# A fused decoder layer on one core: the recurrence's preparation begun 12 slots earlier, its steps spaced wider, and the expert sums cut into four quarters

## The chip, the cores and the metric

One core of a Trainium2 chip runs the whole kernel. The metric is the device time of one execution in microseconds, lower being better. The kernel before took 3550.49 us, the median of three runs (3546.98 to 3573.14).

## What is computed

One decoder layer over 1024 tokens of width 1024, all in float32:

```python
a = rms_norm(h, norm_mix_g)
z = a @ w_in                                   # columns: recurrence 1792, convolution 1024, gates 2048
o_r = rwkv7_branch(z_rwkv, ...)                # recurrence over time, 8 heads of 64
o_c = conformer_conv_branch(z_conv, ...)       # 31 taps, depthwise, layer norm, silu
h = h + (g_r * o_r + g_c * o_c) @ w_out
# expert part: per token 8 heads x 16 chosen experts out of 16384
coef = gates * gelu(einsum('cd,ced->ce', c, u_tab[idx]))
h = h + einsum('ce,ced->cd', coef, v_tab[idx])
h = h + sigmoid(rms_norm(h) @ ple_w_gate) * (p @ ple_w_proj)
return rms_norm(h, final_norm_g)
```

Before the recurrence its inputs are prepared: decay and `a` through small up-projections and sigmoids, the normed key direction `kk`, the running sums of the decay's logarithm inside a chunk of 64 tokens and their exponentials, and a bonus term. The recurrence itself is solved chunk by chunk with matrix products (an inverse of a triangular matrix by squaring), 16 steps for each chunk.

## The kernel before

The 1024 tokens are 8 tiles of 128. The main loop has 10 periods `t` of 128 slots `s` (`SLOTS`), one slot for each expert row of a token. In period `t`:

- GpSimd gathers, in each slot, one row of 4 KB for each of 128 tokens out of `u_tab` for tile `t` (`gather_u`, L986) and one out of `v_tab` for the tile before (`gather_v`, L994, 12 slots late). Each gather is 512 KB. It waits until the buffer it goes to is free; there are 4 to 6 buffers for u and 5 to 8 for v.
- VectorE multiplies the u row with the tile's activations and sums it (`dot`, L2248), one in each slot. Slot 0 of a period is where its first `dot` stands, and the 128 `dot`s mark the slots in the trace.
- TensorE adds one v row block in each slot (`add_tokens`, L1325). The product has 32 output rows, so it fills one of four strips of 32 columns of the array and 32 partitions of the accumulator `acc`. Each is made as two halves of 512 columns, the second on the strip `lane ^ 2`. At the end of a tile VectorE adds `acc` to the residual, putting the strips back in place (`summed`, L2257, slot 12, `SUM_ROWS`).
- Between these, the next tile's front is computed, spread over the same slots by tables and constants (`front(t + 1, s)` on each engine). The preparation (`prep`) stands in slots 0 to 17 (`PREP_AT` for VectorE; slots 2, 5, 9 on TensorE; slots 0, 3, 6, 8, 12 on ScalarE). The recurrence (`rec`) stands in slots 20 to 63: two chunks of 15 entries, one entry each 1.5 slots (`rec_step`), TensorE and ScalarE in the entry's slot and VectorE in the one behind. The 124 convolution taps (`conv_tap`, L1968) of tiles 3 to 7 stand partly (44, `EARLY_TAPS`) one a slot from slot 84 of the period before, the other 80 in slots 0 to 65. From slot 66 come the mixing products with streamed weights, w_out, the turned activations, the queries (slots 104 to 113) and the first scores.
- In periods 1 to 3 TensorE also computes the input projection of the last 512 tokens (`late_product`, L1413). In period 7 there is no front; the tails of the first tiles (gate product, final norm) stand in its place. Periods 8 and 9 only add v rows and do the last tails.

Every engine runs its instructions strictly in the order in which the loops write them, so a wait in one slot holds all that stands behind it on that engine. What ties the engines together are the gathers: the u gather of slot `s` waits for a `dot` some slots back, the v gather for an `add_tokens` some slots back, and both stand in one queue on GpSimd.

The preparation's `p_kk` and `p_nrm` lie in `actT` before, where the next tile's queries read too; `pi` is the PSUM tile `pd` (two banks of 512), which preparation, recurrence, queries and mixing share.

```python
def rec_step(s):
    j = -(-2 * (s - REC_AT) // 3)
    return divmod(j, REC_PE - 1) if s >= REC_AT and j < REC_STEPS and REC_AT + 3 * j // 2 == s else None
```

## Time and profile before

| | us |
|---|---|
| median of 3 runs (lowest to highest) | 3550.49 (3546.98 to 3573.14) |
| the profiled execution's own time | 3567.71 |
| its span, first to last instruction | 3566.0 |
| TensorE busy | 2750.9 (77%) |
| VectorE busy | 2363.7 (66%) |
| GpSimd busy | 1964.6 (55%) |
| ScalarE busy | 531.5 (15%) |
| bytes moved, mean rate | 1246.47 MB, 350 GB/s |
| mean granted TensorE clock | 0.855 |

The profiled execution is 1.71 us longer than its span and 17 us longer than the median of the runs. Busy times are of one engine's own instructions; waits are not in them. By the starts of the `dot`s, periods 0 to 7 begin at 243, 544, 968, 1394, 1799, 2186, 2583 and 2974 us of the span, and the last `dot` starts at 3331 us. In the views, stretches given by start and end in us are stretches of slots found in that way.

### The profile page before, as it was taken

How to read it: one execution, taken by the hardware profiler on the slowest of the kernel's cores; microseconds unless marked ns; L12 is line 12 of the kernel's file. 1: busy time of each engine (PE TensorE's matmuls, PEld its weight loads, DVE VectorE, ACT ScalarE, POOL GpSimd, SP SyncE). 2: the span in 40 equal slices, each digit the busy share in tenths (PEclk: the TensorE clock that was granted, in tenths of full speed). 3: DMA queues.
4: the chain of work that ended last, by engine and by line, in shares of the span. 5: the costliest groups of instructions: out<-in, count | busy, mean ns of one | idle time of the engine just before them, and what ended most of it. 6: DMA issues, size and time to landing. Idle time of an engine off the chain costs nothing.

```text
span 3566.0 us, 42043 instructions
## 1 busy us (share of the span) xinstructions
PE 2750.9 (77%) x15556; PEld 1288.3 (36%) x15556; DVE 2363.7 (66%) x6100; ACT 531.5 (15%) x1162; POOL 1964.6 (55%) x2093
## 2 busy tenths in 40 slices
PE   9899886888888889986756676667656777677787
PEld 7777762333323333333323332233223332222111
DVE  5678889676676657766787767867686756665200
ACT  3211311110111102111011101010111101111101
POOL 0013345555655566556665666666665666666663
PEclk9999997999999899998867786678767787798999
DMA  6559998999999999989999999999999999999996
GB/s 218 209 179 306 352 344 305 329 359 377 382 357 322 366 375 377 369 317 403 393 373 335 369 406 368 353 338 407 379 363 332 394 395 403 386 378 396 375 361 234
DMA packets 385293, 1246.47 MB, mean 350 GB/s; under 512 B 40512, under 2 KB 75072, under 8 KB 384320
## 3 DMA queue, kind: packets, MB, share of 16 engines
q0 software_dynamic: 294912, 1073.87, 79.8%
q1 hardware_dynamic: 90176, 169.91, 13.5%
q8 instruction: 123, 2.02, 0.2%
q14 instruction: 82, 0.67, 0.1%
HBM read 1216.75 MB, written 26.87 MB: 349 GB/s over the span
## 4 chain that ended last, share of the span: by engine, by line
PE 36%; DVE 17%; another core or an unknown queue 13%; DMA 13%; issue 11%; POOL 7%; ACT 2%; SPq 0%; POOLq 0%; DVEq 0%; ACTq 0%
PE e_acc L1325 9%; DVE e_u L2248 5%; PE e_pl L1413 5%; DMA e_v<-in_v_tab,e_idxT 4%; DMA e_u<-in_u_tab,e_idx 3%; PE e_pd L1201 3%; PE e_pd L1021 3%; PE e_pd L1227 3%; PE e_acc L1370 3%; POOL e_v L994 3%; PE e_acc L1395 3%; DVE e_late L2248 2%; POOL e_u L986 2%; DMA e_late<-in_v_tab,e_idxT 2%
## 5 line engine op out<-in xcount | busy, mean ns | idle before, releaser
L2248 DVE CUSTOM_DVE_ANT_0 e_u<-e_u,e_c 128x1024 f32<-128x1024 f32 x776 | 942.4, 1215 | 315.8 <-DMA e_u<-in_u_tab,e_idx 240.4
L986 POOL DMA_INDIRECT e_u<-in_u_tab,e_idx x776 | 745.7, 961 | 693.3 <-DVE e_dots L2248 274.6
L994 POOL DMA_INDIRECT e_v<-in_v_tab,e_idxT x711 | 675.6, 950 | 517.4 <-PE e_acc L1325 203.3
L1325 PE MATMUL e_acc<-e_v,e_wd 128*32 128x512 f32 x2844 | 817.3, 699 | 171.6 <-DMA e_v<-in_v_tab,e_idxT 115.0
L1413 PE MATMUL e_pl<-e_late,e_v 128*128 128x512 f32 x608 | 340.8, 658 | 46.5 <-DVE e_side L2058 17.2
L2248 DVE CUSTOM_DVE_ANT_0 e_late<-e_late,e_c 128x1024 f32<-128x1024 f32 x248 | 300.8, 1214 | 102.4 <-DMA e_late<-in_u_tab,e_idx 74.3
L1325 PE MATMUL e_acc<-e_late,e_wd 128*32 128x512 f32 x832 | 271.9, 731 | 73.5 <-DMA e_late<-in_v_tab,e_idxT 47.2
L986 POOL DMA_INDIRECT e_late<-in_u_tab,e_idx x248 | 237.1, 956 | 163.8 <-DVE e_dots L2248 106.2
L1325 PEld LDWEIGHTS e_acc<-e_v,e_wd 128*32 128x32 f32 x2844 | 113.6, 116 | 533.0 <-issue 266.9
L1968 DVE SCALAR_TENSOR_TENSOR e_gbc<-e_hc,e_cw,e_gbc 128x128 f32<-128x128 f32 x960 | 303.6, 344 | 1.5 <-issue 1.0
L994 POOL DMA_INDIRECT e_late<-in_v_tab,e_idxT x208 | 197.3, 948 | 133.2 <-issue 52.8
L1021 PE MATMUL e_pd<-e_arena 64*64 64x64 f32 x3584 | 164.1, 247 | 117.7 <-ACT e_arena L1479 61.3
L1021 PEld LDWEIGHTS e_pd<-e_arena 64*64 64x64 f32 x3584 | 140.2, 156 | 241.2 <-ACT e_arena L1479 105.1
L1413 PEld LDWEIGHTS e_pl<-e_late,e_v 128*128 128x128 f32 x608 | 98.9, 195 | 296.4 <-issue 241.4
L1479 ACT ACTIVATE e_arena<-e_pd 128x512 f32<-128x512 f32 (+1 forms) x192 | 90.5, 471 | 745.4 <-remote 392.0
L1395 PE MATMUL e_acc<-e_v 128*128 128x256 f32 x608 | 153.6, 396 | 19.9 <-DMA e_v<-in_w_in 15.7
L1201 PE MATMUL e_pd<-e_w_out,e_actT 128*128 128x512 f32 x256 | 135.8, 661 | 23.6 <-DVE e_actT L2121 17.7
L1227 PEld LDWEIGHTS e_pd<-e_actT,e_w_q 128*128 128x128 f32 x1024 | 129.5, 204 | 56.2 <-issue 54.0
L1251 PE MATMUL e_ps<-e_keys,e_qT 64*128 64x128 f32 x256 | 78.8, 395 | 89.7 <-remote 60.2
L1227 PE MATMUL e_pd<-e_actT,e_w_q 128*128 128x128 f32 x1024 | 140.3, 293 | 9.5 <-issue 8.9
L1288 PE MATMUL e_pd<-e_w_out,e_actT 128*128 128x512 f32 x256 | 129.5, 637 | 13.1 <-ACT e_actT L1530 12.2
L1395 PEld LDWEIGHTS e_acc<-e_v 128*128 128x128 f32 x608 | 114.9, 197 | 44.2 <-issue 17.1
(299 smaller groups left out, 3249.4 us busy)
## 6 DMA issues: line engine op xcount, KB each, us to landing
e_u<-in_w_in SPq DMA_DIRECT2D x38, 512.0 KB, 3.9
e_v<-in_w_in SPq DMA_DIRECT2D x38, 512.0 KB
e_v<-in_w_in SPq DMA_DIRECT2D x76, 256.0 KB
e_u<-in_u_tab,e_idx POOLq DMA_INDIRECT x776
e_zb<-in_w_c SPq DMA_DIRECT2D x48, 256.0 KB
e_v<-in_v_tab,e_idxT POOLq DMA_INDIRECT x711
e_arena<-in_w_r SPq DMA_DIRECT2D x32, 256.0 KB
e_zb<-in_w_r SPq DMA_DIRECT2D x32, 256.0 KB
```

Source lines behind the costliest of these rows:

```text
L986: pool.indirect_dma_start(out=rows_in[i], out_offset=None, in_=io["u_tab"], in_offset=bass.IndirectOffsetOnAxis(ap=idx[n % 2][:, j:j + 1], ...
L994: pool.indirect_dma_start(out=rows_in[i], out_offset=None, in_=io["v_tab"], in_offset=bass.IndirectOffsetOnAxis(ap=idxT[n % (LAG + 1)][:, ...
L1021: last = pe.matmul(pi[r, out, i * CH:(i + 1) * CH], a[r, i, :], b[r, i, :] if len(b.shape) == 3 else b[r, :], start=True, stop=True)
L1201: last = pe.matmul(pd[:, h * HALF:(h + 1) * HALF], mixt[:, k, :], w_out[:, k, h * HALF:(h + 1) * HALF], start=(k == 0), stop=(k == KT - 1))
L1227: last = pe.matmul(pd[:, h * P:(h + 1) * P], w_q[:, k, h * P:(h + 1) * P], actT[:, k, :], start=(k == 0), stop=(k == KT - 1))
L1288: last = pe.matmul(pd[:, h * HALF:(h + 1) * HALF], actT[:, k, :], w_ple[:, k, h * HALF:(h + 1) * HALF], start=(k == 0), stop=(k == KT - 1))
L1325: last = pe.matmul(acc[rows, cols], w[:, at_:at_ + 32], rows_in[row][:, cols], start=(step == 0), stop=True, skip_group_check=True)
L1370: last = pe.matmul(out, w_a[m % UW][:, k, :], ahead[:, k, 0:n], start=(k == 0), stop=(k == KT - 1))
L1395: last = pe.matmul(acc[:, first:first + BEHIND_T], w_b[i % BW][:, j, :], behind[:, j, :], start=(j == 0), stop=(j == KT - 1))
L1413: last = pe.matmul(pl[:, :], w_late[:, half, in_half, :], late[:, k, :], start=(k == 0), stop=(k == KT - 1))
L1968: dve.scalar_tensor_tensor(out=out, in0=hc[:, i, j:j + P], scalar=col(cw, j * CONV_TILES + i), in1=out, op0=ALU.mult, op1=ALU.add).then_in ...
L2248: dve.tensor_tensor_reduce(rows_in[i], rows_in[i], c[:, :], 1.0, 0.0, ALU.mult, ALU.add, dots[n % 2][:, j:j + 1]).then_inc(s_dot, 1)
```

## The change

Four things are changed together.

1. The preparation of tiles 2 to 7 begins in slot 116 of the period before its old place (`EARLY = 12`): `prep_at(t + 2, s - SLOTS + EARLY)` at the end of each period, and `prep_at(n, s + begins_early(n))` in `front`. Its own order is changed too: the squared key's norm is made first on TensorE, then the reciprocals, then the scans. It is spread over slots 0 to 20 of its own count (`PREP_DVE_AT`), so 12 of them lie before the period's start and the rest in slots 0 to 8. Tiles 0 and 1 keep their period. `p_kk` goes to the arena and `p_nrm` to `zb`, so that neither lies in `actT`. VectorE has 30 instructions for it, not 29.
2. The recurrence of tiles 2 to 7 starts in slot 10, not 20, and still ends in slot 63: its 30 entries are 53/29 = 1.83 slots apart, not 1.5. For tile 1 it runs from slot 22 to 63.
3. `EARLY_TAPS` goes from 44 to 64, two a slot from slot 84 to 115 instead of one a slot from 84 to 127, so 60 instead of 80 are left for slots 0 to 65 of tiles 3 to 7.
4. `add_tokens` makes each v block as four quarters of 256 columns on the four strips (`strip_of` is `lane ^ part`), not two halves of 512 on two. `summed` puts them back with 11 additions (1 of 128 partitions, 4 of 32, 2 of 64, 4 of 32, each 256 wide), not 3 of 512, and the first `add_tokens` of a tile waits for 5 and then for all 11 of them.

```diff
-PREP_AT = {0: 0, 4: 1, 5: 2, 6: 3, 7: 4, 8: 5, 9: 6, 10: 7, 11: 8, 12: 9, 14: 10, 16: 11, 17: 12}
-REC_AT, REC_STEPS = 20, 2 * (REC_PE - 1)
+EARLY = 12
+PREP_PE_AT = {1: 0, 3: 1, 14: 2}
+PREP_ACT_AT = {0: 0, 2: 1, 4: 2, 7: 3, 10: 4}
...
+REC_AT, REC_END, REC_STEPS = 22, 63, 2 * (REC_PE - 1)
-EARLY_AT, EARLY_TAPS = 84, 44
+EARLY_AT, EARLY_TAPS = 84, 64
...
-SUM_ROWS = [((slice(0, P), slice(0, P)),), ((LOW, HIGH), (HIGH, LOW))]
+SUM_ROWS = [((slice(0, P), slice(0, P)),), tuple((STRIPS[i], STRIPS[i ^ 1]) for i in range(LANES)),
+            ((LOW, HIGH), (HIGH, LOW)), tuple((STRIPS[i], STRIPS[i ^ 3]) for i in range(LANES))]
...
+def rec_step(n, s):
+
+    first = REC_AT - begins_early(n)
+    span, last = REC_END - first, REC_STEPS - 1
+    j = -(-(s - first) * last // span)
+    return divmod(j, REC_PE - 1) if 0 <= j <= last and first + span * j // last == s else None
...
-        return range(min(s - EARLY_AT, EARLY_TAPS), min(s - EARLY_AT + 1, EARLY_TAPS)) if s >= EARLY_AT else range(0)
+        return range(min(2 * (s - EARLY_AT), EARLY_TAPS), min(2 * (s - EARLY_AT + 1), EARLY_TAPS)) if s >= EARLY_AT else range(0)
...
-        p_kk, p_nrm = actT[:, 0:PAIRS, :], actT[:, PAIRS:, :]
+        p_kk, p_nrm = part(30, 4, "p (i t) -> p i t", i=PAIRS), zb[:, :, 0, :, 0, :]
...
-                for h in range(D // HALF):
+                for h in range(PARTS):
                     if j == 0 and n:
-                        pe.wait_ge(s_hh, SUMS[NH] * (n - 1) + SUMS[h + 1])
-                    cols = slice(h * HALF, (h + 1) * HALF)
+                        pe.wait_ge(s_hh, SUMMED * (n - 1) + (HALF_SUMMED, SUMMED)[h * PART_W // HALF])
+                    cols = slice(h * PART_W, (h + 1) * PART_W)
...
                     if t + 1 < NT:
                         front(t + 1, s)
+                    if t + 2 < NT and s >= SLOTS - EARLY:
+                        prep_at(t + 2, s - SLOTS + EARLY)
```

VectorE in slots 117 to 121 of period 5. L2248 is the dot (two rows of it in each slot), L1968 a tap, L2156 to L2172 the choice of the best 16 of a head. Before:

```order
L2156 MATCH_REPLACE e_sc<-e_tv,e_sc 128x128
L2157 MATCH_REPLACE e_sc<-e_tv,e_sc 128x128
L2248 ISA e_u,e_dots<-e_u,e_c 128x1024
L2248 ISA e_dots 128x1
L1968 SCALAR_TENSOR_TENSOR e_gbc<-e_hc,e_cw,e_gbc 128x128
L2162 MAX e_tv<-e_sc 128x8 x2
L2248 ISA e_late,e_dots<-e_late,e_c 128x1024
L2248 ISA e_dots 128x1
L1968 SCALAR_TENSOR_TENSOR e_gbc<-e_hc,e_cw,e_gbc 128x128
L2166 MAX_INDEX e_ti<-e_tv,e_sc 128x8 x2
L2167 TENSOR_TENSOR e_onehot<-e_tv 128x256
```

The same engine after, slots 116 to 120 (L2291 is the dot, L1939 to L1947 the preparation of tile 7: the key direction, the norm's lower bound, a reciprocal):

```order
L1939 TENSOR_TENSOR e_arena<-e_arena,e_vec 128x512
L2291 ISA e_u,e_dots<-e_u,e_c 128x1024
L2291 ISA e_dots 128x1
L2232 TENSOR_SCALAR e_half<-e_pos 128x16 x2
L2291 ISA e_u,e_dots<-e_u,e_c 128x1024
L2291 ISA e_dots 128x1
L2235 CAST e_halff<-e_half 128x32
L1943 TENSOR_SCALAR e_zb<-e_pd 128x2x4x64
L2291 ISA e_u,e_dots<-e_u,e_c 128x1024
L2291 ISA e_dots 128x1
L2238 TENSOR_TENSOR e_onehot<-e_halff,e_iota 128x512
L1947 RECIPROCAL e_zb<-e_zb 128x2x64
```

The taps have left these slots and the preparation's instructions have come in.

TensorE from the start of a period on. L1215 turns the activations for the new tile's dots, L1135, L1152 and L1156 are the preparation, L1325 the v sums. Before:

```order
L1325 MATMUL e_acc<-e_v,e_wd 32x512 x4
L1215 MATMUL e_c<-e_ident,e_actT 128x128 x8
L1325 MATMUL e_acc<-e_v,e_wd 32x512 x6
L1135 MATMUL e_pd<-e_arena,e_wa_up 128x128 x8
L1325 MATMUL e_acc<-e_late,e_wd 32x512 x4
L1325 MATMUL e_acc<-e_v,e_wd 32x512 x2
L1251 MATMUL e_ps<-e_keys,e_qT 128x128 x2
L1135 MATMUL e_pd<-e_arena,e_g_up 128x128 x4
L1152 MATMUL e_pd<-e_actT,e_headones 128x512
```

After (L1232 turns the activations, L1163 and L1152 are the preparation, L1349 the v sums):

```order
L1163 MATMUL e_pd<-e_zb,e_headones 128x512
L1152 MATMUL e_pd<-e_arena,e_wa_up 128x128 x4
L1349 MATMUL e_acc<-e_late,e_wd 32x256 x4
L1349 MATMUL e_acc<-e_v,e_wd 32x256 x4
L1268 MATMUL e_ps<-e_keys,e_qT 128x128 x2
L1152 MATMUL e_pd<-e_arena,e_wa_up 128x128 x4
L1152 MATMUL e_pd<-e_arena,e_g_up 128x128 x4
L1349 MATMUL e_acc<-e_v,e_wd 32x256 x16
L1349 MATMUL e_acc<-e_late,e_wd 32x256 x8
L1349 MATMUL e_acc<-e_v,e_wd 32x256 x8
L1232 MATMUL e_c<-e_ident,e_actT 128x128 x8
```

All but one product of the preparation now stand ahead of the period's start, and a v block is four products of 256 columns, not two of 512.

VectorE at the sum of a tile, slot 12, after (L1895 is the recurrence's first step, L2300 the sum); before, the sum is one row of 128x512 and one of 64x512 x2, and the recurrence has not begun:

```order
L1895 TENSOR_TENSOR e_arena<-e_pd,e_m_g 128x512 x2
L2300 TENSOR_TENSOR e_x<-e_x,e_acc 128x256
L2300 TENSOR_TENSOR e_x<-e_x,e_acc 32x256 x4
L2300 TENSOR_TENSOR e_x<-e_x,e_acc 64x256 x2
L2300 TENSOR_TENSOR e_x<-e_x,e_acc 32x256 x4
L2291 ISA e_u,e_dots<-e_u,e_c 128x1024
```

The sum has 11 instructions in place of 3, and stands right behind the recurrence's first VectorE step.

## Rows read from the trace of the kernel before

**Rows 1.** The page: GB/s in 40 slices of the span.

```profile
GB/s 218 209 179 306 352 344 305 329 359 377 382 357 322 366 375 377 369 317 403 393 373 335 369 406 368 353 338 407 379 363 332 394 395 403 386 378 396 375 361 234
```

**Rows 2.** Windows of period 5, slots from 0, 8, 24, 84, 116; then slots 80 to 87.

```profile
core 0: us, PE busy (x) PEld busy (x) DVE busy (x) ACT busy (x) POOL busy (x), PEclk, DMA share, GB/s
2186.00:2215.00 29.00, 19.14 (x73) 7.41 (x65) 21.63 (x55) 7.57 (x18) 20.18 (x21) 0.61 0.97 353
2215.00:2266.00 51.00, 23.79 (x119) 10.12 (x120) 43.94 (x110) 3.24 (x9) 31.95 (x34) 0.64 1.01 387
2266.00:2398.00 132.00, 86.30 (x864) 42.88 (x860) 89.87 (x255) 15.71 (x39) 79.31 (x85) 0.75 0.94 333
...
2452.00:2538.00 86.00, 68.40 (x287) 28.62 (x285) 61.38 (x149) 5.29 (x17) 54.94 (x58) 0.85 1.02 400
2538.00:2583.00 45.00, 25.18 (x103) 7.23 (x103) 23.80 (x65) 5.80 (x9) 29.58 (x33) 0.67 1.00 382
...
2440.00:2462.00 22.00, 17.37 (x104) 8.86 (x96) 15.37 (x47) 0.00 (x0) 14.86 (x16) 0.92 1.03 411
```

**Rows 3.** Slots 24 to 65: periods 1, 2, sum of 1 to 6, then 7.

```profile
619.00:765.00 146.00, 124.66 (x956) 49.03 (x954) 105.22 (x304) 21.41 (x51) 79.31 (x85) 0.94 0.93 333
1046.00:1192.00 146.00, 125.33 (x947) 50.55 (x944) 92.64 (x258) 17.73 (x42) 78.22 (x85) 0.91 0.92 327
...
sum 839.00, PE 635.14 PEld 278.32 DVE 558.79 ACT 104.25 POOL 479.50; mean PE 105.86 PEld 46.39 DVE 93.13 ACT 17.37 POOL 79.92
...
3033.00:3165.00 132.00, 83.61 (x279) 26.43 (x280) 78.27 (x199) 20.03 (x45) 87.85 (x91) 0.78 1.00 380
```

**Rows 4.** Waits of DVE, 2266 to 2398 us: us in total, times, longest.

```profile
DVE e_arena L1869 <- remote: 11.0, 3, 6.3
DVE e_arena L1878 <- remote: 10.3, 1, 10.3
DVE e_arena L1878 <- PE e_pd L1107: 9.9, 1, 9.9
DVE e_arena L1869 <- PE e_pd L1021: 5.4, 1, 5.4
DVE e_arena L1872 <- ACT e_arena L1479: 3.2, 1, 3.2
```

**Rows 5.** Timeline: v sums, one block, one block, two blocks at once.

```profile
1852.80 1.05 PE L1325 MATMUL e_acc<-e_v,e_wd 128*32 128x512 f32 x4 [1.93 <-DMA e_v<-in_v_tab,e_idxT]
...
1856.67 1.92 PE L1325 MATMUL e_acc<-e_v,e_wd 128*32 128x512 f32 x4 [1.25 <-DMA e_v<-in_v_tab,e_idxT]
...
1872.04 1.07 PE L1325 MATMUL e_acc<-e_late,e_wd 128*32 128x512 f32 x2
...
1872.05 1.07 PE L1325 MATMUL e_acc<-e_v,e_wd 128*32 128x512 f32 x2
```

**Rows 6.** VectorE groups by form: line, engine, op, count, busy us, mean ns.

```profile
L1968 DVE SCALAR_TENSOR_TENSOR e_gbc<-e_hc,e_cw,e_gbc 128x128 f32<-128x128 f32 x960 | 303.6, 344 | 1.5 <-issue 1.0
L1928 DVE RECIPROCAL e_actT<-e_actT 128x128 f32<-128x128 f32 x32 | 29.9, 938 | 0.0
L1910 DVE TENSOR_TENSOR_SCAN e_arena<-e_ones,e_arena 128x64 f32<-128x64 f32 x64 | 12.7, 269 | 13.0 <-ACT e_arena L1558 10.6 <-issue 2.4
L1945 DVE TENSOR_TENSOR e_zb<-e_arena 64x512 f32<-64x512 f32 x16 | 11.0, 686 | 0.3
L1875 DVE TENSOR_TENSOR e_arena<-e_pd,e_arena 128x256 f32<-128x256 f32 x16 | 6.7, 419 | 23.1 <-PE e_pd L1021 16.3 <-remote 6.5 <-issue 0.3
```

**Rows 7.** Windows: slots 0 to 7 of period 1; slots 116 to 127 of period 0.

```profile
544.00:566.00 22.00, 8.46 (x32) 6.04 (x33) 21.97 (x51) 9.24 (x21) 10.07 (x11) 0.50 0.64 198
...
515.00:544.00 29.00, 13.05 (x63) 10.88 (x61) 21.00 (x55) 5.34 (x9) 12.28 (x13) 0.75 1.00 367
```

**Rows 8.** Window of the whole of period 7.

```profile
2974.00:3331.00 357.00, 256.12 (x818) 73.19 (x818) 224.25 (x519) 58.53 (x127) 238.26 (x248) 0.83 1.00 387
```

**Rows 9.** Timeline: the last tile's sum.

```profile
3535.74 2.12 DVE L2257 TENSOR_TENSOR e_x<-e_x,e_acc 128x512 f32<-128x512 f32 x3 [130.38 <-PE e_acc L1325]
```

More of the change, by code:

```diff
@@ L160 @@
 LOW, HIGH = slice(0, P // 2), slice(P // 2, P)
-SUM_ROWS = [((slice(0, P), slice(0, P)),), ((LOW, HIGH), (HIGH, LOW))]
-SUMS = [sum(len(r) for r in SUM_ROWS[:h]) for h in range(NH + 1)]
+STRIP = P // LANES
+PARTS = LANES
+PART_W = D // PARTS
+STRIPS = [slice(STRIP * i, STRIP * (i + 1)) for i in range(LANES)]
+SUM_ROWS = [((slice(0, P), slice(0, P)),), tuple((STRIPS[i], STRIPS[i ^ 1]) for i in range(LANES)),
+            ((LOW, HIGH), (HIGH, LOW)), tuple((STRIPS[i], STRIPS[i ^ 3]) for i in range(LANES))]
+SUMS = [sum(len(r) for r in SUM_ROWS[:h]) for h in range(PARTS + 1)]
+SUMMED, HALF_SUMMED = SUMS[PARTS], SUMS[PARTS // 2]
 TAIL_AT, TAIL_SPAN, EARLY_TAILS = 4, 20, NT - 1 - LAG
@@ L169, in token_at, with strip_of @@
     return (P // LANES) * (k % LANES) + k // LANES
-def strip_of(lane, h):
-    return lane ^ (2 * h)
+def strip_of(lane, part):
+    return lane ^ part
 ROWS = UW + VW + LW + 2
@@ L1302, in ple_proj, with begins @@
                 product(pt, w_proj, PLE // P, 1, out).then_inc(s_pps, 1)
+            begun = set()
+            def begins(n, strip, bank):
+                first = (n, strip, bank) not in begun
+                begun.add((n, strip, bank))
+                return first
             def add_tokens(n, j, together):
@@ L1322, in add_tokens, with prep_at @@
                         strip = strip_of(lane, h)
-                        rows = slice(32 * strip, 32 * strip + 32)
+                        rows = STRIPS[strip]
                         at_ = (step % QUARTER) * P + 32 * lane
-                        last = pe.matmul(acc[rows, cols], w[:, at_:at_ + 32], rows_in[row][:, cols], start=(step == 0), stop=True,
+                        last = pe.matmul(acc[rows, cols], w[:, at_:at_ + 32], rows_in[row][:, cols],
+                                         start=begins(n, strip, h * PART_W // HALF), stop=True,
                                          skip_group_check=True)
-                        if h == D // HALF - 1:
+                        if h == PARTS - 1:
                             last.then_inc(s_vmm, 1)
+            def prep_at(n, s):
+                if s in PREP_PE_AT:
+                    prep(n, PREP_PE_AT[s])
             def front(n, s):
-                if s in (2, 5, 9):
-                    prep(n, (2, 5, 9).index(s))
-                r = rec_step(s)
+                prep_at(n, s + begins_early(n))
+                r = rec_step(n, s)
                 if r:
@@ L1905, in prep @@
                 if k == 1:
-                    dve.wait_ge(s_pa, n_a + 9)
-                    for i in range(PAIRS):
+                    dve.wait_ge(s_pp, n_p + 1)
+                    dve.wait_ge(s_wu, 2 * KT * n)
+                    done(dve.tensor_scalar(p_nrm, pi[:, 0, :].rearrange("p (c i t) -> p c i t", c=2, i=PAIRS), 1e-24, None, ALU.max))
+                if 2 <= k < 2 + PAIRS:
+                    own(2)
+                    ch, i = divmod(2 * (k - 2), PAIRS)
+                    done(dve.reciprocal(p_nrm[:, ch, i:i + 2, :], p_nrm[:, ch, i:i + 2, :]))
+                if k in (6, 7):
+                    dve.wait_ge(s_pa, n_a + 13)
+                    for i in (2 * (k - 6), 2 * (k - 6) + 1):
                         for ch in range(2):
@@ L2253, in summed @@
                 dve.wait_ge(s_vmm, (n + 1) * NSEL)
-                for h in range(D // HALF):
-                    cols = slice(h * HALF, (h + 1) * HALF)
+                for h in range(PARTS):
+                    cols = slice(h * PART_W, (h + 1) * PART_W)
                     for rows, from_ in SUM_ROWS[h]:
```

135 lines of the change are left out of this document (72 added, 63 removed).

## The prediction

> **What bounds the kernel now.** I read the page's rates first. From the tenth slice on, when both gathers run, the core moves between 317 and 408 GB/s, and the slices alternate [rows 1]. The reader is to see a ceiling and dips under it. To find where the dips are I cut each period at slots and read the windows. In period 5 slots 80 to 87 move 411 GB/s, the highest rate of any such window, with VectorE busy 15.37 of 22 us; slots 84 to 115 move 400, slots 8 to 23 387, and slots 24 to 65 only 333 [rows 2]. I call the time that a stretch's bytes would need less at 411 GB/s its gap: us x (1 - rate/411). For slots 24 to 65 of period 5 that is 132 x (1 - 333/411) = 25.1 us. The same slots of periods 1 and 2 have 27.7 and 29.8, and of period 7, which has no front and so no recurrence, 132 x (1 - 380/411) = 10.0 [rows 3]. Periods 1 to 6 spend 839 us there [rows 3]; at their mean rate of 333 the gap is 839 x 0.190 = 159 us. All other stretches of period 5 have little: 4.1 in slots 0 to 7, 3.0 in 8 to 23, 2.3 in 84 to 115, 3.2 in 116 to 127 [rows 2]. So the kernel runs near its transfer rate except where the recurrence stands and little is to be had elsewhere.
>
> Why the transfers stop there is in the waits. VectorE is idle 132 - 89.87 = 42.1 us of that stretch, and 39.8 of it are five groups of waits on recurrence steps (L1869, L1872, L1878), with no wait for a gathered row among them [rows 4]. A dot stands behind each such wait, a u buffer behind the dot, and the next gather behind the buffer. TensorE is busy 86.30 of 132 us [rows 2], and it alternates between recurrence products and v sums. In periods 1 and 2, with the late products, it is busy 125 of 146 [rows 3], and the gap is only 3 to 5 us larger: TensorE's load alone is not the cause, the chain of steps across the engines is. 27 of the 30 entries stand in these 42 slots: 132/27 = 4.9 us for each, of which VectorE waits 42.1/27 = 1.56.
>
> **The change part by part.** The times are of the profiled execution (3567.71 us, span 3566.0, 17 us over the median of the runs); the sum is a difference, which I take off both.
>
> *Steps 1.83 slots apart.* 22 entries instead of 27 stand in slots 24 to 65. With the same wait for each, VectorE is idle 22 x 1.56 = 34 us. Its work there falls by 13 taps of 0.344 [rows 6], 4.5 us, and by about 2 us for the steps that left, to 83.4. Together 117.7 instead of 132, still above what 411 GB/s needs (107). That is 14 us less. The bounds: nothing, if TensorE and VectorE stay out of step whatever the spacing (a wait of 10 us at L1878 [rows 4] is longer than three slots, so spacing alone does not cover it), and 22 us, if only the gap that other stretches have (3 in 50 us) is left.
>
> *v sums in quarters.* One block takes 1.05 us at 1852.80 and 1.92 us at 1856.67, where the clock was lower; at 1872.04 two blocks, four strips, start within 0.01 us of each other and each part lasts as long as one alone, 1.07 [rows 5]. So four strips run at once, and four quarters of half the columns should take some 0.6 and 1.06 us: 0.45 to 0.86 less for each block. The bounds are no gain (twice the instructions, if their issue decides) and half. In the 42 slots of period 5 TensorE has 42 x 0.6 = 25 us less to do out of 86. Most of that becomes idle time, since it waits for the chain too; where a block stands between a step and the next engine, the chain gets shorter. I count 1 us in a period in the recurrence, for about two of VectorE's waits, so 15 us in all there: 6 x 15 = -90. In period 7, rate 387 over 357 us [rows 8], gap 21 us, tails and v sums share TensorE (256 us busy): I take a quarter, -5. Between nothing and -15.
>
> *Preparation 12 slots earlier.* Of its VectorE work these move to slots 116 to 127: four instructions of 512 columns at 0.686, four reciprocals at 0.938, eight scans at 0.269, and the lower bound of the norm, 0.69 [rows 6]: 2.74 + 3.75 + 2.15 + 0.69 = 9.3 us. Slots 0 to 23 lose them and get the recurrence's first eight entries instead of three. VectorE was busy 43.94 of 51 us in slots 8 to 23 [rows 2]; there it loses some 9.9 us of the preparation and 1.7 of taps, gets 1.9 of steps and of the rest of the preparation, 2.6 of the longer sum and 5 x 1.56 = 7.8 of new waits: 44.6, under the 48 that the transfers need. No gain there and no loss. Slots 0 to 7 have a gap of 4.1 us in period 5 and of 22 x (1 - 198/411) = 11.4 in period 1 [rows 2, 7], with the preparation's first waits in them; I take 1 us a period back, 6 x -1 = -6, between 0 and -15.
>
> What it costs at the other end: TensorE now waits in slot 117 for ScalarE's square, which waits for VectorE's product of slot 116, behind two activations with their table loads. Queued behind it on TensorE are the v sums of slots 118 on, and GpSimd's gathers wait for these. The same wait stood in slot 2 before, so it moves and is not new. VectorE in slots 84 to 127 of period 5 is busy 61.38 + 23.80 = 85 of 131 us [rows 2]; it gets 20 taps (6.9 us) and 9.3 us of preparation: 101 of 131. Nearest is the stretch of slots 8 to 23, busy 86% with a gap of 6%; slots 84 to 127 have 5.5 in 131 now, 4.2%. Going to 6% is 2.5 us, in five periods, and 3 us in period 0, where VectorE was busy 21.00 of 29 us [rows 7] and must take 30.3: +15.5 in all. The bounds are 0 and 11.4 us a period (the first slots of period 1 carried over).
>
> *The sum of a tile.* 11 instructions of 256 columns at 0.42 [rows 6] are 4.6 us; before, three took 2.12 [rows 9]. The partitions do not enter: 64 take 0.686 for 512 columns and so would 128. In slot 12 of periods 2 to 7 the 2.5 us more on VectorE are mostly hidden by the room worked out above; I take 0.5 each, +3. For the last tile nothing hides them: +2.5.
>
> The z load that the preparation needs is issued some 30 slots ahead of slot 116; POOL's queue and SP's have the same rows in the same order. Tile 1's recurrence (slots 22 to 63) and its preparation cost nothing: TensorE's input projection fills that period.
>
> Sum: -90 - 5 - 6 + 15.5 + 5.5 = -80 us. 3567.7 - 80 = 3488 for an execution like the profiled one, and 3550.5 - 80 = 3470.5, so 3471, for the median.
>
> **The rivals.** *The chain goes on as before (3535).* The long waits at L1878 come because VectorE runs slots ahead of TensorE, not because entries are close. Then the recurrence gives only its taps, 3 us a period, -18, with -6, -5 and +21 elsewhere is -8; 1 us a period from the quarters makes it -14 to -15: 3535. For it: these two waits are half of the 42 us [rows 4]. Against: each entry is a trip across three engines, and in 4.9 us TensorE must also fit 1.5 v sums of 1 to 1.9 us, which shrink.
>
> *TensorE's clock.* The granted clock is 0.91 to 0.94 in slots 24 to 65 of periods 1 and 2, with the engine busy 85%, and 0.72 to 0.75 in period 5 with 65% [rows 2, 3]. With shorter v sums the first could come to the second's level (0.5 of the full 2.4 GHz is the lower level, 1.2). The other work of a period there, some 85 us at 0.93, would take 85 x 0.93/0.74 = 107: the 22 us that the quarters save are given back. That takes the three periods with late products out of part of the gain: -80 + 3 x 10 = -50, 3500. The Trainium skill ("TensorE: Matmul & The Clock Gate", Part 1: The HAM clock gate) says that the clock follows how busy the array has been of late, so that less work can mean slower work; the trace agrees, in the two granted clocks just read. Against its deciding: in period 5 the gap is no larger at 0.75 than in periods 1 and 2 at 0.91 to 0.94.
>
> *The gap nearly closes (3415).* If the steps at 1.83 slots always find their inputs, the recurrence keeps a gap of 3 us a period: 159 - 18 = -141, with -5 - 15 for first slots and period 7 and +25 for the rest: -136. For it: slots 84 to 115 run at 400 GB/s with TensorE busier (68 of 86 us) than here [rows 2].
>
> *The end of the period becomes the bound (3600).* VectorE and the wait in slot 117 hold slots 84 to 127 as the first slots of period 1 were held: 11.4 us of gap in each of six periods, +68; two taps a slot cost +3 more in five periods, +15; the sum's 2.5 us are exposed on eight tiles, +20. The chain stays (-18 for taps), and the first slots and the quarters give back at most their bounds, -15 and -15. 68 + 15 + 20 - 18 - 30 = +55, with 5 off for what overlaps, +50: 3600. It decides from 14 us a period on, where it eats the gain. For it: period 1's first slots at 198 GB/s [rows 7]. Against: VectorE there was busy 21.97 of 22 us, and here it would be 78%.
>
> **How the numbers follow.** Forecast 0.46, the clock's fall 0.12, chain as before 0.17, gap nearly closed 0.17, end of period 0.08. The forecast's own range is 3440 to 3510. The whole range must take most of the neighbours: 3405 to 3545. A measurement of this kernel can tell about 1% from no change, 35.5 us, so faster means under 3515: 0.45 of the forecast, 0.10 of the clock's case, 0.17 of the closed gap and 0.03 of the chain's case make 0.75. The rest of these, 0.01 + 0.02 + 0.14, is 0.17 for the same, and the last case is 0.08 for slower.
>
> **What would show each step.** In windows of slots 24 to 65 the rate goes from 333 to about 370 GB/s and the us from 132 to 117; VectorE's waits on the recurrence from 42 us to 30. A v block's four rows last 0.6 or 1.06 us. Slots 8 to 23 keep their 50 us with VectorE less busy. Slots 84 to 127 take 2 to 3 us more. The sum of the last tile is 4.6 us. The prediction is wrong if the 10 us waits at L1878 stay, if TensorE's clock falls by over 0.15 in periods 1 to 3 and the us there do not fall, or if slots 116 to 127 lose more than 5 us a period.

## The result and the profile after

The changed kernel takes 3594.23 us (median of 4 runs, 3591.49 to 3599.95) beside 3551.05 for the kernel before (4 runs, 3546.98 to 3573.14): a ratio of 1.0093, 95% interval 1.0066 to 1.012. The medians themselves are 43 us, 1.2%, apart; the ratio of the record is not theirs, and with four runs a side the loss is best read as about 1%. I had forecast 3471 and a range of 3405 to 3545. The profiled execution has a span of 3589.8 us, 23.8 more than that of before. Before's was 17 us over the median of its runs and this one is 3 under, so the profiles show 24 of the 43 us. The page, total busy time, granted clock and rates of after, beside [rows 1]:

```profile
PE 2598.3 (72%) x19652; PEld 1433.6 (40%) x19652; DVE 2377.1 (66%) x6172; ACT 541.3 (15%) x1168; POOL 1975.9 (55%) x2093
...
PEclk9999997888989899987767786768666777878798
...
GB/s 217 198 187 311 350 349 277 333 380 376 369 346 339 378 383 383 360 349 405 370 353 343 374 404 344 349 362 409 369 347 337 406 403 391 387 352 375 363 347 220
```

The same ceiling, the same dips. TensorE is busy 2598 us instead of 2751, at a mean granted clock of 0.821 instead of 0.855. The windows of period 5 of after, slots 0 to 7, 8 to 23, 24 to 65, 116 to 127, against [rows 2]:

```profile
2191.00:2213.00 22.00, 10.38 (x69) 4.38 (x72) 21.79 (x50) 1.02 (x4) 14.93 (x16) 0.59 0.97 357
2213.00:2268.00 55.00, 31.06 (x316) 17.83 (x308) 37.45 (x103) 3.64 (x9) 31.50 (x34) 0.64 0.91 340
2268.00:2400.00 132.00, 86.55 (x901) 50.37 (x901) 86.03 (x241) 13.26 (x33) 81.18 (x86) 0.68 0.95 345
...
2538.00:2580.00 42.00, 25.63 (x189) 14.82 (x188) 27.51 (x69) 15.52 (x26) 27.84 (x29) 0.72 0.97 362
```

Slots 24 to 65 still take 132 us. Slots 8 to 23 fell from 387 to 340 GB/s, with VectorE less busy (37.45 us for 43.94). The same for slots 24 to 65 of period 1, their sum over periods 1 to 6, and the whole of period 7, against [rows 3, 8]:

```profile
622.00:764.00 142.00, 115.27 (x1004) 50.49 (x1002) 103.77 (x299) 16.96 (x42) 82.82 (x86) 0.87 0.95 345
...
sum 815.00, PE 595.07 PEld 296.81 DVE 540.65 ACT 88.72 POOL 486.93; mean PE 99.18 PEld 49.47 DVE 90.11 ACT 14.79 POOL 81.15
...
2973.00:3346.00 373.00, 234.31 (x1338) 88.63 (x1330) 225.05 (x527) 58.68 (x127) 244.34 (x252) 0.77 0.98 373
```

Cut at the dots of these slots, in both traces, the balance is: periods 1 to 6 are 23 us shorter in slots 24 to 65 (838 to 815) and 18 in slots 0 to 7, and 26 longer in slots 8 to 23 (314 to 340) and 13 in slots 116 to 127 (243 to 256); their total is 2426 us for 2430, so what the middle slots gained was lost around them. Period 7 takes 16 more and the stretch behind the last dot 9 more (235 to 244). VectorE's waits of after in slots 24 to 65 of period 5 (us in total, times, longest), against [rows 4]:

```profile
DVE e_arena L1913 <- remote: 12.4, 1, 12.4
DVE e_arena L1913 <- PE e_pd L1124: 9.6, 1, 9.6
DVE e_arena L1907 <- ACT e_arena L1509: 6.3, 1, 6.3
DVE e_arena L1904 <- remote: 5.5, 1, 5.5
```

L1913 is the old L1878. Its waits of about 10 us stayed, one of the three things that I had said would prove the prediction wrong. What makes slots 8 to 23 longer stands in the timeline of VectorE and TensorE around the dots of slots 11 and 12 (start, us, instruction, idle before):

```profile
2214.62 2.15 PE L1051 MATMUL e_pd<-e_zb 64*128 64x128 f32 x16
2216.70 0.64 PE L1349 MATMUL e_acc<-e_v,e_wd 128*32 128x256 f32 x8
...
2218.81 1.23 DVE L2291 CUSTOM_DVE_ANT_0 e_u<-e_u,e_c 128x1024 f32<-128x1024 f32 x1
...
2228.43 1.29 DVE L1895 TENSOR_TENSOR e_arena<-e_pd,e_m_g 128x512 f32<-128x512 f32 x2 [7.98 <-remote]
2229.63 4.90 DVE L2300 TENSOR_TENSOR e_x<-e_x,e_acc 128x256 f32<-128x256 f32 x11
2229.77 1.97 PE L1060 MATMUL e_pd<-e_zb 64*64 64x64 f32 x32 [12.43 <-DVE e_arena L1895]
2234.56 1.22 DVE L2291 CUSTOM_DVE_ANT_0 e_late<-e_late,e_c 128x1024 f32<-128x1024 f32 x1
```

TensorE's first recurrence step (L1051) is over at 2216.77 by its records. VectorE's step on it (L1895) starts at 2228.43, 11.7 us later, idle for 8, and TensorE's next step waits 12.43 for that. The releaser is "remote": the profile shows no instruction that ended then, though the semaphore update of L1051 itself is recorded there, at 2228.40. Behind it stand the sum of tile 4 in 11 instructions (4.90 us) and the dot of slot 12. From dot to dot that is 15.8 us; in the same place of before's profile it was 6.9, with a wait of 2.12 us ahead of the sum:

```profile
2227.81 2.12 DVE L2257 TENSOR_TENSOR e_x<-e_x,e_acc 128x512 f32<-128x512 f32 x3 [2.12 <-remote]
```

Over periods 2 to 7 the dots of slots 11 and 12 stand 81 us apart in all, for 37 before. Periods 1 to 6 are no longer for it, so a wait here is not by itself time of the kernel.

My first theory (Q) was that the quarters are the loss (period 7 and the end have no front), and its rival (F) that the front's new places are.

### The profile page after: what moved, and what is told of

Same layout as the page of the kernel before. It is cut to its first block, busy times and chain, and to the rows that moved or that the text cites. A ratio compares the mean times of both kernels' runs of the same rounds, so it can differ in the third digit from the quotient of the medians.

```text
span 3589.8 us, 50313 instructions
## 1 busy us (share of the span) xinstructions
PE 2598.3 (72%) x19652; PEld 1433.6 (40%) x19652; DVE 2377.1 (66%) x6172; ACT 541.3 (15%) x1168; POOL 1975.9 (55%) x2093
## 4 chain that ended last, share of the span: by engine, by line
PE 14%; another core or an unknown queue 13%; DVE 13%; issue 12%; DMA 5%; POOL 5%; ACT 1%; SPq 0%; POOLq 0%; DVEq 0%; ACTq 0%
PE e_acc L1349 4%; DVE e_u L2291 4%; PE e_pd L1244 2%; POOL e_v L1011 2%; DVE e_late L2291 2%; DMA e_v<-in_v_tab,e_idxT 2%; DMA e_u<-in_u_tab,e_idx 1%; DMA e_late<-in_u_tab,e_idx 1%; PE e_pl L1441 1%; PE e_pd L1218 1%; PE e_pd L1038 1%; PE e_pd L1305 1%; POOL e_late L1011 1%; POOL e_u L1003 1%
## 5 line engine op out<-in xcount | busy, mean ns | idle before, releaser
L2291 DVE CUSTOM_DVE_ANT_0 e_u<-e_u,e_c 128x1024 f32<-128x1024 f32 x776 | 942.5, 1215 | 262.4 <-DMA e_u<-in_u_tab,e_idx 182.6
L1349 PE MATMUL e_acc<-e_v,e_wd 128*32 128x256 f32 x5688 | 643.2, 462 | 210.7 <-DMA e_v<-in_v_tab,e_idxT 106.8
L1349 PEld LDWEIGHTS e_acc<-e_v,e_wd 128*32 128x32 f32 x5688 | 187.2, 122 | 573.5 <-issue 360.9
L1441 PE MATMUL e_pl<-e_late,e_v 128*128 128x512 f32 x608 | 356.4, 684 | 67.1 <-DVE e_side L2101 25.9
L2291 DVE CUSTOM_DVE_ANT_0 e_late<-e_late,e_c 128x1024 f32<-128x1024 f32 x248 | 300.6, 1214 | 90.2 <-DMA e_late<-in_u_tab,e_idx 70.1
L1349 PE MATMUL e_acc<-e_late,e_wd 128*32 128x256 f32 x1664 | 228.1, 482 | 77.6 <-DMA e_late<-in_v_tab,e_idxT 38.1
L1038 PE MATMUL e_pd<-e_arena 64*64 64x64 f32 x3584 | 175.7, 251 | 117.1 <-issue 64.6
L1218 PE MATMUL e_pd<-e_w_out,e_actT 128*128 128x512 f32 x256 | 138.0, 670 | 27.9 <-DVE e_actT L2164 23.9
L2300 DVE TENSOR_TENSOR e_x<-e_x,e_acc 32x256 f32<-32x256 f32 (+2 forms) x88 | 36.7, 418 | 162.8 <-PE e_acc L1349 134.3
L1349 PEld LDWEIGHTS e_acc<-e_late,e_wd 128*32 128x32 f32 x1664 | 69.8, 126 | 178.0 <-issue 108.0
```

The lines of the kernel that those rows point to most:

```text
L1038: last = pe.matmul(pi[r, out, i * CH:(i + 1) * CH], a[r, i, :], b[r, i, :] if len(b.shape) == 3 else b[r, :], start=True, stop=True)
L1218: last = pe.matmul(pd[:, h * HALF:(h + 1) * HALF], mixt[:, k, :], w_out[:, k, h * HALF:(h + 1) * HALF], start=(k == 0), stop=(k == KT - 1))
L1349: last = pe.matmul(acc[rows, cols], w[:, at_:at_ + 32], rows_in[row][:, cols], start=begins(n, strip, h * PART_W // HALF), stop=True, skip ...
L1441: last = pe.matmul(pl[:, :], w_late[:, half, in_half, :], late[:, k, :], start=(k == 0), stop=(k == KT - 1))
L2291: dve.tensor_tensor_reduce(rows_in[i], rows_in[i], c[:, :], 1.0, 0.0, ALU.mult, ALU.add, dots[n % 2][:, j:j + 1]).then_inc(s_dot, 1)
```

## The experiments

The ratios are to the kernel before on the same chip, with 95% intervals. The times fell on two levels of the kernel before, about 3354 us and about 3586; 3551 of the result is near the slower. Runs made together stayed at one level. The expectations speak of faster and slower kinds of chip; the chip of runs 7 to 10 and that of runs 17 and 18 have one number and different levels, so I keep to "level".

**1, 2: quarters alone; all without quarters.** Run 1 is the kernel before with the changed v sums and sum. Run 2 is the changed kernel with `SUM_ROWS` of before and

```diff
-PARTS = LANES
+PARTS = D // HALF
...
-    return lane ^ part
+    return lane ^ (2 * part)
```

> The kernel before with one part of the change: v sums as four quarters on four strips, with the tile sum in 11 instructions; preparation, recurrence and taps stay where they were. Theory Q (the quarters are what costs: the changed kernel loses 16 us in period 7 and 9 us behind the last dot, stretches that have no front and that only the quarters and the sum touch): about +25 to +43 us on the kernel before, 3576 to 3594, with the granted clock near 0.82 and period 7 at about 373 us. Theory F (the front's new places are what costs, the quarters give what I predicted): 20 us or more below the kernel before, about 3530, with period 7 at 350 or less. Theory R (neither alone: the recurrence's chain does not care): within 10 us of the kernel before.

> The changed kernel with v sums in halves on two strips and the sum in three instructions again; early preparation, steps 1.83 slots apart and two taps a slot stay. Theory Q: the loss goes; at or below the kernel before, 3535 to 3555, with period 7 back at 357 us and 235 us behind the last dot. Theory F: no better than the changed kernel, 3594 to 3615, since the v blocks are longer again. Theory R: between them, near 3570, with slots 8 to 23 at 57 us a period and slots 24 to 65 at about 137 as in the changed kernel.

Measured at the faster level: 1.0020 (1.0009 to 1.0031) and 1.0016 (1.0007 to 1.0025). Neither theory's size appears: run 1 is 5 us over the kernel before, which the third (R) had, within 10.

**3, 4: preparation and taps alone; taps alone.** Run 3 is run 2 with `first = 20 if n > 1 else REC_AT` for the steps; run 4 is the kernel before with `EARLY_TAPS = 64`, two a slot.

> As the run without quarters, but tiles 2 to 7 take their recurrence steps in slots 20 to 63, 1.48 slots apart, as the kernel before does; only preparation and taps are early. If early steps in slots 10 to 23 are what lengthened slots 8 to 23 (from 52 to 57 us a period), this one has 50 to 52 us there and 140 in slots 24 to 65, and the comparison with the run without quarters gives the price of the spacing: theory F has this one 10 to 20 us faster than that run, my prediction has it some 60 us slower, theory R within 10 us of it. If the preparation in slots 116 to 127 itself costs (these slots took 257 us in the changed kernel against 242), this one is 10 us or more above the kernel before.

> The kernel before with 64 early taps, two a slot, instead of 44, one a slot; nothing else. My prediction: the end of the period loses nothing or 2.5 us at most, the recurrence's stretch gains 3 to 4 us a period at VectorE, so between 0 and -20 us. If VectorE's work in slots 24 to 65 does not decide (the waits on the steps grow by what the taps leave free), it is within 5 us of the kernel before; a rival that makes the doubled taps delay the dots of slots 84 to 115 has it 5 to 15 us slower.

Measured: 1.0010 (1.0000 to 1.0019) and 1.0001 (0.9992 to 1.0010). Run 3 against run 2 is the test of the steps alone, from slot 20 and 1.48 slots apart against from 10 and 1.83: my prediction had run 3 some 60 us slower, and it is 2 to 4 us faster, no difference beyond the intervals. In the profiles slots 24 to 65 of periods 1 to 6 take 686 us in run 3 and 685 in run 2. Run 4 is in effect a profile of the kernel before at the faster level: slots 24 to 65 of its period 5, and VectorE's waits in them.

```profile
2127.00:2237.00 110.00, 76.27 (x867) 35.05 (x868) 89.06 (x242) 14.84 (x37) 80.34 (x86) 0.95 1.03 408
```

```profile
DVE e_u L2248 <- DMA e_u<-in_u_tab,e_idx: 12.7, 21, 1.5
DVE e_late L2248 <- DMA e_late<-in_u_tab,e_idx: 6.1, 10, 1.0
DVE e_arena L1872 <- ACT e_arena L1479: 0.3, 1, 0.3
```

This is the main reading of the study. The steps stand 1.5 slots apart, as before, and the stretch that I called bound by their chain runs at 408 GB/s in 110 us. VectorE waits for gathered rows and 0.3 us for a step, not 39.8. There was no gap for the change to close at this level. At the slower one the gap isn't made by the spacing either: runs 8 and 9 below differ in the same way, and by less than 0.1%.

**5, 6: both kernels again.** No edit.

> The changed kernel itself, unaltered, beside the kernel before on a chip of the experiments. The four runs so far were on a chip where the kernel before takes 3354 us instead of 3551 and moves 408 GB/s in slots 24 to 65 of periods 4 to 6, where the other chip's profile shows 333. Theory T (transfers cap this chip, so no part of the change can win and each costs only what it takes from the free-running stretches): parts add up, 1.002 for the quarters and 1.0016 for the rest, so 3364 to 3368, a ratio of 1.003 to 1.005. Theory Q+F (the parts hurt each other, as the first steps and the long sum meet in slots 11 and 12): a ratio of 1.009 as on the first chip, 3384. If the transfers are no cap and my prediction's mechanism holds: under 3340.

> The kernel before itself, unaltered, for a profile on the chip of the experiments. If the delays of the first chip are a matter of that chip and not of the program, no semaphore update of a recurrence step comes more than 2 us behind the end of its matmul's record (64 such delays, 244 us in all, in the profile of before on the first chip), the time is within 5 us of 3354, and VectorE's waits at L1869 and L1878 in slots 24 to 65 are under 20 us a period instead of 40. If the program makes them, they are here too.

Both ran at the slower level: 1.0076 (1.0051 to 1.0102) for the changed kernel, so the result repeats on another chip, and 3590.06 us for the kernel before. Its profile shows how the slower level looks. ScalarE and TensorE in slot 27 of period 5:

```profile
2283.18 1.90 PE L1021 MATMUL e_pd<-e_arena 64*64 64x64 f32 x32 [4.31 <-ACT e_arena L1479]
2285.01 1.88 PE L1325 MATMUL e_acc<-e_late,e_wd 128*32 128x512 f32 x4
```

```profile
2288.55 0.60 ACT L1479 ACTIVATE e_arena<-e_pd 128x512 f32<-128x512 f32 x1 [5.42 <-remote]
```

The squares end at 2285.08 and ScalarE reads them at 2288.55. In run 4 the same pair is this, 0.05 us apart:

```profile
2147.97 1.15 PE L1021 MATMUL e_pd<-e_arena 64*64 64x64 f32 x32
2149.17 0.60 ACT L1479 ACTIVATE e_arena<-e_pd 128x512 f32<-128x512 f32 x1 [13.14 <-PE e_pd L1021]
```

I compared in each trace the recorded end of each of TensorE's steps with its semaphore update, from period 1 on. Over 2 us late are 64 in before's profile (244 us in all), 73 in after's (344), 66 in run 6 and 81 in run 5, and none in any of the ten profiles at the faster level (runs 1 to 4, 11 to 14, 17, 18).

The profiles differ in one thing more. Those at the slower level lack over 40% of the semaphore updates themselves: before's has 27502 of them, run 4's 47855, and the ten at the slower level have 25718 to 27502, the ten at the faster 47769 to 47873. So "remote" can stand for an update that is missing as well as for one that came late, and it is open whether the recording of the profile is what slows an execution at this level, since none is known to have run without it.

**7 to 10: the parts at the slower level, and the sum alone.** Runs 7, 8, 9 repeat 1, 2, 3. Run 10 is the kernel before with the sum cut in 11, halves as before:

```diff
-SUM_ROWS = [((slice(0, P), slice(0, P)),), ((LOW, HIGH), (HIGH, LOW))]
+S4 = [slice(32 * i, 32 * i + 32) for i in range(4)]
+SUM_ROWS = [[((slice(0, P), slice(0, P)),), tuple((r, r) for r in S4)],
+            [((LOW, HIGH), (HIGH, LOW)), tuple((S4[i], S4[i ^ 2]) for i in range(4))]]
...
-                    cols = slice(h * HALF, (h + 1) * HALF)
-                    for rows, from_ in SUM_ROWS[h]:
+                  for q in range(2):
+                    cols = slice(h * HALF + 256 * q, h * HALF + 256 * (q + 1))
+                    for rows, from_ in SUM_ROWS[h][q]:
```

> The same kernel as the run with quarters alone (ratio 1.002 on a chip where the kernel before takes 3354 us), for a chip of the slower kind, where it takes 3551 or 3586, TensorE's semaphore updates come up to 12 us late and the whole change costs 0.76 to 0.93%. Theory Q (the quarters are the loss): a ratio of 1.007 to 1.010 on the slower kind. Theory S (the early steps are, 5 to 6 us a period in slots 8 to 23): within 0.3% of 1 there, with slots 8 to 23 at 50 to 53 us and 8 to 10 us more behind the last dot and its sum. If the chip is of the faster kind: 1.001 to 1.003 again.

> The same kernel as the run without quarters (ratio 1.0016 on the faster kind of chip), for a chip of the slower kind. Theory Q: a ratio of 1.000 or below there, slots 8 to 23 at 52 us. Theory S: 1.007 to 1.010, slots 8 to 23 at 57 us and slots 24 to 65 near 135. Theory D (both are paid for through the number of late updates: 73 of over 2 us in the changed kernel against 64): between, 1.003 to 1.006 each, and each with more late updates than the kernel before.

> The same kernel as the run with early preparation and taps alone (ratio 1.001 on the faster kind of chip), for a chip of the slower kind. Theory S: the loss goes with the early steps, so 1.000 to 1.002 there, 0.6% below the run without quarters. Theory Q and D: within 0.2% of the run without quarters. If the preparation itself in slots 116 to 127 is the loss, 1.005 or more here too.

> The kernel before, with the sum of a tile in the changed kernel's 11 instructions of 256 columns, but v sums in halves. My prediction: 2.5 us more on VectorE in each of 8 tiles, of which 0.5 each in periods 2 to 7 and 2.5 for the last tile are seen, so +3 to +6 us (0.1 to 0.2%) on either kind of chip. The rival's price, exposed on all eight tiles: +20 (0.6%). If the quarters' loss is their sum, this run has all of it; if it is TensorE's side, this run is within 0.1%.

Measured, one chip: quarters 1.0061 (1.0045 to 1.0077), without quarters 0.9977 (0.9963 to 0.9990), preparation and taps alone 0.9985 (0.9969 to 1.0001), the sum alone 1.0041 (1.0024 to 1.0058). So Q holds against F here, with a loss of quarters a little under the 1.007 it asked for: the schedule is worth 8 us and the quarters cost 22. The sum alone costs 15, two thirds of that by the middle values; the intervals of runs 7 and 10 overlap, so what is left for TensorE's side of the quarters isn't told apart from nothing. S, which blamed the early steps, had run 8 at 1.007 or more and fails. D, which paid through the number of late updates, fails too: by the same comparison run 8 has over 80 of them (some 390 us, the most of any profile) and is the fastest here, run 9 has 53. Where it goes, run 6 first (three instructions), then run 10, the dots of slots 11 and 12 of period 5 around the sum:

```profile
2231.41 1.22 DVE L2248 CUSTOM_DVE_ANT_0 e_u<-e_u,e_c 128x1024 f32<-128x1024 f32 x1
...
2233.97 2.12 DVE L2257 TENSOR_TENSOR e_x<-e_x,e_acc 128x512 f32<-128x512 f32 x3
...
2236.12 1.22 DVE L2248 CUSTOM_DVE_ANT_0 e_late<-e_late,e_c 128x1024 f32<-128x1024 f32 x1
```

```profile
2229.80 1.21 DVE L2250 CUSTOM_DVE_ANT_0 e_u<-e_u,e_c 128x1024 f32<-128x1024 f32 x1
...
2232.36 4.78 DVE L2260 TENSOR_TENSOR e_x<-e_x,e_acc 128x256 f32<-128x256 f32 x11
2237.16 1.22 DVE L2250 CUSTOM_DVE_ANT_0 e_late<-e_late,e_c 128x1024 f32<-128x1024 f32 x1
2237.18 0.18 PEld L1327 LDWEIGHTS e_acc<-e_late,e_wd 128*32 128x32 f32 x4 [2.49 <-DVE e_x L2260]
```

4.7 us become 7.4 from dot to dot, 2.7 for the 2.66 that the sum is longer, and TensorE's first block of the next tile waits for it too. Yet periods 1 to 6 take 2441 us in both profiles: slots 8 to 23 give 9 more, slots 116 to 127 take 20 less, and such a stretch moves by as much between two profiles of one kernel. What stays is the end. Behind the last dot it is 235 us in both profiles of the kernel before, 236 in run 8 and 238.5 in run 9, all with the sum in three, but 247 in runs 7 and 10 and 244 to 248 in those of the changed kernel and of run 15, all with the sum in 11; at the faster level it is 222 to 225 and 228 to 230. So 9 to 12 of the 15 us are there. Two sums stand in that stretch, tile 6's some 18 to 23 us behind the last dot and the last one; in run 10 the last v sum ends 9 us later than in run 6, and the last sum is 2.7 longer.

**11 to 14: steps behind the sum.** Alone the parts come to -0.23% and +0.61%, +0.38% together, yet the whole costs 0.76 and 0.93%. Theory M: the first step and the long sum meet in slot 12. Run 11 is the changed kernel, run 12 run 2, both with

```diff
-    first = REC_AT - begins_early(n)
+    first = 14 if n > 1 else REC_AT
```

Run 13 is the changed kernel, run 14 run 2.

> The changed kernel with one number changed: the first recurrence step of tiles 2 to 7 stands in slot 14 instead of slot 10, so all steps come behind the tile sum of slot 12 and stand 1.69 slots apart; quarters, preparation and taps stay. Theory M (the meeting in slot 12 is what makes the parts cost more together than alone: from the dot of slot 11 to that of slot 12 it is 4.7 us in the kernel before, 7.4 with the long sum, 15 to 17.6 in the changed kernel): on a chip of the slower kind 0.3 to 0.5% faster than the changed kernel, a ratio to the kernel before near 1.004, and slot 12 at 7 to 9 us. Rival G (the wait only moves to where the first step then stands, and the clock of TensorE is what the quarters lose): within 0.15% of the changed kernel. On a chip of the faster kind both give a ratio of 1.002 to 1.004.

> The run without quarters with the same first step in slot 14. Without quarters it stood at 0.9977 of the kernel before on a chip of the slower kind, with 7.5 to 14.6 us at slot 12. Theory M: slot 12 at 4 to 5 us and a ratio of 0.995 to 0.997. Rival G: 0.9977 again within 0.15%. On a chip of the faster kind: 1.000 to 1.0016.

> The changed kernel itself again, to stand on the same chip as the three others of this call. On a chip of the slower kind 1.0076 to 1.0093 as twice before; on a chip of the faster kind the parts would add up to 1.0035 or so (1.002 for quarters, 1.0016 for the rest).

> The run without quarters again, for the same comparison. If the quarters, with their sum, cost no more in the changed kernel than alone (0.61% on the slower kind of chip), it is 0.6% below the changed kernel; theory M has it 0.9 to 1.1% below. On a chip of the faster kind: 0.2% below.

Measured, all at the faster level: 0.9966 (0.9954 to 0.9978), 1.0006 (0.9997 to 1.0015), 0.9993 (0.9985 to 1.0002) and 1.0017 (1.0008 to 1.0026). The changed kernel is no slower here; with its steps from slot 14 on it is 0.34% faster than the kernel before, which none of my expectations had. Nor had they run 13, expected near 1.0035, or run 14, expected 0.2% below it and measured 0.24% above. The slot 12 of period 5 in run 13, the changed kernel, with the wait gone:

```profile
2094.15 1.21 DVE L2291 CUSTOM_DVE_ANT_0 e_u<-e_u,e_c 128x1024 f32<-128x1024 f32 x1
...
2095.69 1.26 DVE L1895 TENSOR_TENSOR e_arena<-e_pd,e_m_g 128x512 f32<-128x512 f32 x2
2096.88 4.90 DVE L2300 TENSOR_TENSOR e_x<-e_x,e_acc 128x256 f32<-128x256 f32 x11
...
2101.80 1.22 DVE L2291 CUSTOM_DVE_ANT_0 e_late<-e_late,e_c 128x1024 f32<-128x1024 f32 x1
```

7.65 us from dot to dot: the same instructions, without the 8 us of idle time.

**15, 16: the same two at the slower level.**

> The changed kernel with its first step in slot 14, again, for a chip of the slower kind; on the faster kind it stood at 0.9966 of the kernel before and 0.27% below the changed kernel. Theory M (first step and longer sum meet in slot 12): on the slower kind 0.3 to 0.5% below the changed kernel, 1.003 to 1.006 of the kernel before, with slot 12 at 7 to 9 us instead of 15 to 17.6. Rival G (the wait moves to where the first step stands): within 0.15% of the changed kernel. On the faster kind: 0.9966 again.

> The changed kernel itself beside it on the same chip: 1.0076 to 1.0093 on a chip of the slower kind, 0.9993 on one of the faster.

Measured: 1.0049 (1.0034 to 1.0063) and 1.0089 (1.0073 to 1.0104), 0.40% apart, as M said and G did not. But M's sign failed: in the profile of run 15 slot 12 still takes 15 us, with no step in it:

```profile
2232.25 1.21 DVE L2291 CUSTOM_DVE_ANT_0 e_u<-e_u,e_c 128x1024 f32<-128x1024 f32 x1
...
2242.24 4.91 DVE L2300 TENSOR_TENSOR e_x<-e_x,e_acc 128x256 f32<-128x256 f32 x11 [8.38 <-remote]
...
2247.18 1.22 DVE L2291 CUSTOM_DVE_ANT_0 e_late<-e_late,e_c 128x1024 f32<-128x1024 f32 x1
```

Now the sum itself waits for a late update, that of the last v sums: they end at 2228.91 by their records and the update is recorded at 2242.15. So 0.40% for the place of the first step is measured; that it is the meeting in slot 12 is not shown (this profiled run lies 12 us over its median, run 16's 10 under; their slots 8 to 23 take 338 and 336 us in periods 1 to 6).

**17, 18: two remaining questions.** Run 17 is run 12. Run 18 is the changed kernel with `first = 18`, steps 1.55 slots apart.

> The run without quarters and with the first step in slot 14, again, for a chip of the slower kind (on the faster it stood at 1.0006 of the kernel before). Moving the first step from slot 10 to 14 gave the changed kernel 0.40% there and 0.27% on the faster kind. If it gives the same without the long sum: 0.994 to 0.996 of the kernel before, better than both kernels on that kind of chip. If the gain hung on the long sum beside it: 0.9977 again. On the faster kind: 1.0006 again.

> The changed kernel with its first step in slot 18, so the steps stand 1.55 slots apart, nearly as in the kernel before (1.5). The spacing that my prediction valued at 15 us a period is then gone again. If spacing is worth anything, this run is slower than the one with the first step in slot 14 (1.0049 on the slower kind, 0.9966 on the faster) by 10 us or more; if only the way past slot 12 counted, it is within 0.15% of that run; if later is better still, below it.

Both at the faster level: 1.0008 (0.9999 to 1.0018), as run 12, and 0.9983 (0.9974 to 0.9992). Against run 11, 1.69 slots apart, that is 0.17% or 6 us, on another chip and with intervals that overlap, between the two outcomes that its expectation named (over 10 us, or under 0.15%). So spacing isn't shown to be worth anything here either. What run 12 would be at the slower level stayed open. No version tried is shown to beat both kernels at both levels: run 8 does at the slower, run 11 at the faster (as run 15, at the slower, it is 0.49% over the kernel before).

## Why the prediction was wrong

- **The step that failed is "with the same wait for each, VectorE is idle 22 x 1.56 = 34 us".** It took the 42 us of waits for a cost of each entry of the chain. They come at the slower level alone (39.8 us there, 0.3 in run 4) and don't shrink with the entries: VectorE is idle 132 - 86.03 = 46 us in after's stretch, with 22 entries, for 42 in before's, with 27. With them come late semaphore updates of TensorE, some 52 us in all for the steps of this stretch in either profile and none at the faster level. How much of a wait they make wasn't separated: the 10.3 us wait at L1878 ends with an update that is 2.1 us late, and until then TensorE was still at the steps before it. Of the -90, the profiles give -23 in slots 24 to 65 and +26 in slots 8 to 23; all of the schedule measures -8 us (run 8) at one level and +5 (run 2) at the other, and the place and spacing of its steps nothing beyond the intervals at either (runs 2 and 3, 8 and 9).
- **"No gain there and no loss" in slots 8 to 23** priced each moved entry at 1.56 us. The first one alone waits 8 us at slot 12 of period 5 at the slower level, and not at all in run 13.
- **The quarters.** A block lasts 0.64 us (the row of 8 at 2216.70) or 1.08, as forecast. "In the 42 slots of period 5 TensorE has 25 us less to do" was wrong as time: it is busy 86.55 us for 86.30, at a granted clock of 0.68 for 0.75. In six periods it was 595 for 635. The faster level shows it better: in slots 24 to 65 of period 5 run 14 is busy 75 us at 0.94 and run 13 75 us at 0.70, so the work fell by about a quarter and the clock took all of it. Nor was the time on the path: at the faster level the rows are waited for.
- **The sum.** 4.6 us forecast, 4.9 measured. Its cost was mis-sized: 5.5 forecast, 15 in run 10 (9 to 21 by its interval). "Mostly hidden" for periods 2 to 7 isn't refuted by the profiles; +2.5 for the end is at the slower level, with 9 to 12 (at the faster it is 5: 228.2 in run 13 for 223.6 in run 14). I had counted the last sum alone there, not tile 6's, with TensorE's next block behind it. How the v sums behind it come to end 6 to 9 us late I didn't find.
- **Period 7:** -5 forecast, +16 in the first pair of profiles, +6 in run 5 against run 6, +5 in run 7. That isn't the quarters' doing: run 9, without them, has 369 us, as much as run 16. At the faster level all ten profiles have 343.5 to 344.7, with and without quarters, so the term is nothing.
- **The end of the period** held within its range: +13 us in slots 116 to 127 and -6 in 84 to 115 of periods 1 to 6 in the first pair, -5 and -4 in the second, against +12.5. At the faster level, where profiles of one kernel agree better, early preparation costs 11 us there (221 us in run 3 for 210 in run 4), close to what I had; with quarters beside it there are 212 in run 13. First slots: -18 in the first pair, -1 in the second; the -6 lies between.
- **What stays open.** Schedule and quarters alone come to +14 us at the slower level and the whole to 27 to 43. No run shows what makes the other 13 to 29.
- **The rivals.** The clock fell in periods 1 to 3, from 0.91 to 0.94 to 0.87 to 0.90, by less than I had named. It doesn't decide: at the faster level it is 0.821 in run 13 and 0.90 in run 14, and run 13 is the faster by 0.24%. The Trainium skill's rule on the clock ("TensorE: Matmul & The Clock Gate", Part 1) agrees with the fall; whether a fall costs time is for the runs to say, and here it doesn't. "The chain goes on as before" (3535) had the mechanism for the steps, that spacing doesn't cover these waits, but left the sum at +3. "The end of the period" (3600) had the time, and one term near the measured size, +20 for an exposed sum, which is mostly at the end and not in eight tiles.

## What to carry to other kernels

A wait that follows a product is not yet a cost of the chain: look whether the engine waited for had finished by its own records, and whether the wait shrinks where fewer entries stand. Best is a pair of runs that differ in the steps alone: here runs 2 and 3 show the spacing to be worth nothing. An edit that lengthens one engine's burst is priced where the burst stands, at the next instruction that feeds a transfer, not against the mean room of its stretch. When a forecast rests on a gap under the highest rate, take a second profile at another time, on another chip, first; here such a one had no gap.
